# Weight ring and operands placed on 512-byte multiples, narrow weight tiles 192 bytes beside

## The reference

```python
def first_block(x, ...):              # two layers, post-norm
    for layer in range(2):
        mix = dsa_mixer(h, ...) if layer == 0 else hgrn2_mixer(h, ...)
        h = layer_norm(ALPHA * h + mix, ...)
        h = layer_norm(ALPHA * h + swiglu(h, w_gate, w_up, w_down), ...)

def second_block(x, ...):             # one layer, pre-norm
    proj = rms_norm(x) @ w_in         # split into the parts of GLA and of MLA
    y_a = gla_branch(...) @ w_o_gla
    y_b = mla_branch(...) @ w_o_mla
    mixed = (g_a * y_a + g_b * y_b) @ w_out
    x = x + rms_norm(mixed)
    x = x + rms_norm(swiglu(rms_norm(x)))
```

## The kernel before, in words

| tensor | begins at | modulo 512 |
|---|---|---|
| wh | 16512 | 128 |
| stage, wl | 65664 | 128 |
| x_res, xh, xl, ident | 114816, 123008, 131200, 139392 | 128 |
| arena, and hh, hl, oh, ol, mixed_l, lat_h in it | 151904 and on | 352 |
| lat_l | 224224 | 480 |

## Time and profile before

### The profile page before, as it was taken

How to read it: one execution, slowest core, us unless ns; L and a number is a source line. 1 busy time by engine, 2 the same in 40 slices (tenths; PEclk the granted TensorE clock), 3 DMA queues, 4 the chain that set the end, 5 groups by cost and what they waited for, 6 DMA issues and landing times.

```text
span 1100.5 us, 15631 instructions
## 1 busy us (share of the span) xinstructions
PE 1074.5 (98%) x6604; PEld 939.6 (85%) x6604; DVE 403.0 (37%) x730; ACT 554.4 (50%) x741; POOL 775.8 (70%) x201
## 2 busy tenths in 40 slices
PE   8989999999999998999999999999999999999997
PEld 7867888888889997888888899999999988888886
DVE  5984311118743677511110051821184333111103
ACT  6583453443257876444434256465566356443520
POOL 5623698788578751888888868776675767988880
PEclk9999999999999998999999999999999999999999
DMA  9211665555455431575555446544452555555541
GB/s 364 89 39 43 238 222 187 191 191 183 146 208 191 155 116 58 201 259 191 191 180 172 146 159 227 187 160 149 158 188 78 197 185 211 190 184 173 183 150 39
DMA packets 27446, 186.46 MB, mean 169 GB/s; under 512 B 3168, under 2 KB 3424, under 8 KB 5872
## 3 DMA queue, kind: packets, MB, share of 16 engines
q1 hardware_dynamic: 25184, 178.83, 46.7%
q10 hardware_dynamic: 2192, 6.62, 1.8%
HBM read 184.39 MB, written 1.05 MB: 168 GB/s over the span
## 4 chain that ended last, share of the span: by engine, by line
PE 90%; DVE 7%; ACT 1%; DMA 1%; issue 0%; DVEq 0%; SPq 0%
PE ps L382 28%; PE ps L384 27%; PE ps L383 27%; PE ps L1271 1%; PE ps L1432 1%; DVE arena L1046 1%; PE ps L1136 1%; DMA stage<-in_tiles 1%; DVE arena L2306 1%; DVE arena L1062 1%; DVE arena L890 1%; DVE arena L1057 0%; DVE arena L868 0%; PE ps L2141 0%; PE ps L2142 0%
## 5 line engine op out<-in xcount | busy, mean ns | idle before, releaser
L366 POOL TENSOR_TENSOR wl<-stage,wh 128x2048 fp32r<-128x2048 f32 x166 | 763.5, 4621 | 287.0 <-ACT wh L362 256.9
L362 ACT ACTIVATE wh<-stage 128x2048 fp32r<-128x2048 f32 (+1 forms) x167 | 318.0, 1906 | 113.6 <-DMA stage<-in_tiles 112.9
L382 PE MATMUL ps<-wh,xh 128*128 128x512 f32 (+2 forms) x832 | 306.1, 368 | 0.9 <-DVE xl L1095 0.9
L384 PE MATMUL ps<-wh,xl 128*128 128x512 f32 (+2 forms) x832 | 302.0, 363 | 0.0
L383 PE MATMUL ps<-wl,xh 128*128 128x512 f32 (+2 forms) x832 | 301.7, 363 | 0.0
L382 PEld LDWEIGHTS ps<-wh,xh 128*128 128x128 f32 x832 | 157.3, 189 | 24.7 <-DVE xl L1095 1.2
L384 PEld LDWEIGHTS ps<-wh,xl 128*128 128x128 f32 x832 | 157.0, 189 | 24.9
L383 PEld LDWEIGHTS ps<-wl,xh 128*128 128x128 f32 x832 | 157.3, 189 | 23.2
L382 PE MATMUL ps<-xh,wh 128*128 128x256 f32 x464 | 133.1, 287 | 0.8 <-DVE wl L509 0.8
L384 PE MATMUL ps<-xh,wl 128*128 128x256 f32 x464 | 131.3, 283 | 0.0
L383 PE MATMUL ps<-xl,wh 128*128 128x256 f32 x464 | 131.3, 283 | 0.0
(11 more groups left out here) (379 smaller groups left out, 1171.2 us busy)
## 6 DMA issues: line engine op xcount, KB each, us to landing
stage<-in_tiles SPq DMA_DIRECT2D x167, 1024.0 KB, 4.9
arena<-in_ln_g ACTq DMA_DIRECT2D x4, 512.0 KB, 3.6
arena<-in_ln_b ACTq DMA_DIRECT2D x4, 512.0 KB, 4.9
arena<-in_x_t SPq DMA_DIRECT2D x1, 1024.0 KB, 5.5
x_res<-in_x SPq DMA_DIRECT2D x1, 1024.0 KB, 20.8
out<-x_res SPq DMA_DIRECT2D x4, 256.0 KB, 2.1
stage<-in_tiles SPq DMA_DIRECT2D x1, 544.0 KB, 8.9
arena<-in_pre_mix_norm ACTq DMA_DIRECT2D x1, 512.0 KB, 6.7
```

What stands on the lines that cost most here:

```text
L362: nc.scalar.activation(wh[:, ring(n), part], stage[:, ring(n), part], ACT.Copy).then_inc(hi_done, 1)
L366: nc.gpsimd.tensor_tensor(wl[:, ring(n), :], stage[:, ring(n), :], wh[:, ring(n), :].bitcast(F32), ALU.subtract).then_inc(lo_done, 1)
L382: mm(out_, lh, rh, start=start, stop=False, skip_group_check=skip)
L384: return mm(out_, ll, rh, start=False, stop=stop, skip_group_check=skip)
```

## The change

The descriptor scratch is set to 8192 bytes. `until_line` puts gap tensors ahead of `wh`, of `stage`/`wl`, of `xh` and of `arena`, so that each begins at a multiple of 512 bytes; `x_res` and `xl` then do too, and in the arena `hh`, `hl`, `oh`, `ol`, `mixed_l` and `lat_h`; `lat_l` has remainder 128. A slot of the ring has 2176 instead of 2048 elements (8704 bytes). `tile_of` is now the one way to a tile in its slot: tiles whose number is in `narrow` stand 48 elements (192 bytes) into the slot in `stage`, `wh` and `wl`. No instruction is added, removed or moved, and no size of one changes.

```diff
+SCRATCH, LINE = 8192, 512
 TW = 2048
+ROW = TW + 128
+BESIDE = 48
...
+    at = [SCRATCH + 128]
...
         def sb(name, shape, dt=F32):
+            at[0] = -(-(at[0] + math.prod(shape[1:]) * (2 if dt == BF16 else 4)) // 32) * 32
             return ctx.enter_context(nc.sbuf_tensor(name, shape, dt))
...
+        def until_line(offset):
+
+            gap = (offset - at[0]) % LINE
+            if gap:
+                sb("gap%d" % at[0], [P, gap // 4])
+
+        until_line(0)
+        wh = sb("wh", [P, RING, ROW], F32R)
+        until_line(0)
+        with nc.sbuf_tensor("stage", [P, RING, ROW], F32) as stage:
             pass
-        wl = sb("wl", [P, RING, TW], F32R)
+        wl = sb("wl", [P, RING, ROW], F32R)
+
+        def tile_of(ring_of, n, a=0, b=TW):
+
+            return ring_of[:, n % RING, SHIFT[n] + a:SHIFT[n] + b]
+
         x_res = sb("x_res", [P, 2, D])
+        until_line(0)
         xh = sb("xh", [P, KD, T], F32R)
...
+        until_line(0)
         ARENA = 19360
...
+        narrow = {0, 1, 3, *range(t_hx, t_hwo), *range(t_rest, t_ukv), *range(t_gwo, t_out)}
+        SHIFT = [BESIDE if n in narrow else 0 for n in range(FIRST["end"])]
...
-            sp.dma_start(stage[:, ring(n), :], A["tiles"][n]).then_inc(stage_in[ring(n)], 16)
+            sp.dma_start(tile_of(stage, n), A["tiles"][n]).then_inc(stage_in[ring(n)], 16)
...
-                               (wh[:, s, o:o + P], wl[:, s, o:o + P]), (high[:, x0 + k, :], low[:, x0 + k, :]),
+                               (tile_of(wh, n, o, o + P), tile_of(wl, n, o, o + P)), (high[:, x0 + k, :], low[:, x0 + k, :]),
...
-                               (wh[:, s, o:o + 512], wl[:, s, o:o + 512]), start and k == 0, stop and k == 1, skip=True)
+                               (tile_of(wh, n, o, o + 512), tile_of(wl, n, o, o + 512)), start and k == 0, stop and k == 1, skip=True)
...
-    nc = bacc.Bacc("TRN2", target_bir_lowering=False, num_devices=1)
+    nc = bacc.Bacc("TRN2", target_bir_lowering=False, num_devices=1, dynamic_dma_scratch_size=SCRATCH)
```

More of the change, by code:

```diff
@@ L177, in sem @@
             return ctx.enter_context(nc.semaphore(name))
-        wh = sb("wh", [P, RING, TW], F32R)
-        with nc.sbuf_tensor("stage", [P, RING, TW], F32) as stage:
-            pass
-        wl = sb("wl", [P, RING, TW], F32R)
+        def until_line(offset):
[6 more added lines that the diff above has]
+        with nc.sbuf_tensor("stage", [P, RING, ROW], F32) as stage:
+            pass
+        wl = sb("wl", [P, RING, ROW], F32R)
+        def tile_of(ring_of, n, a=0, b=TW):
+            return ring_of[:, n % RING, SHIFT[n] + a:SHIFT[n] + b]
         x_res = sb("x_res", [P, 2, D])
+        until_line(0)
         xh = sb("xh", [P, KD, T], F32R)
@@ L350, in load @@
             if n == 1:
-                sp.dma_start(stage[:, 1, 0:KD * IW], A["tiles"][1, :, 0:KD * IW]).then_inc(stage_in[1], 16)
+                sp.dma_start(tile_of(stage, 1, 0, KD * IW), A["tiles"][1, :, 0:KD * IW]).then_inc(stage_in[1], 16)
                 return
-            sp.dma_start(stage[:, ring(n), :], A["tiles"][n]).then_inc(stage_in[ring(n)], 16)
+            sp.dma_start(tile_of(stage, n), A["tiles"][n]).then_inc(stage_in[ring(n)], 16)
         def ring(n):
@@ L360, in hi @@
             act.wait_ge(stage_in[ring(n)], come[n])
-            part = slice(0, KD * IW if n == 1 else TW)
-            nc.scalar.activation(wh[:, ring(n), part], stage[:, ring(n), part], ACT.Copy).then_inc(hi_done, 1)
+            part = (0, KD * IW if n == 1 else TW)
+            nc.scalar.activation(tile_of(wh, n, *part), tile_of(stage, n, *part), ACT.Copy).then_inc(hi_done, 1)
         def lo(pool, n):
             pool.wait_ge(hi_done, n + 1)
-            nc.gpsimd.tensor_tensor(wl[:, ring(n), :], stage[:, ring(n), :], wh[:, ring(n), :].bitcast(F32),
-                                    ALU.subtract).then_inc(lo_done, 1)
+            nc.gpsimd.tensor_tensor(tile_of(wl, n), tile_of(stage, n), tile_of(wh, n).bitcast(F32), ALU.subtract
+            ).then_inc(lo_done, 1)
         his = [1]
@@ L396, in tile_a @@
             low_ready(pe, n)
-            s = ring(n)
             high, low = src or (xh, xl)
@@ L423, in tile_b @@
                     last = mm3(out_, (xh[:, k, x], xl[:, k, x]),
-                               (wh[:, s, o:o + cols], wl[:, s, o:o + cols]), k == 0, k == kt - 1)
+                               (tile_of(wh, n, o, o + cols), tile_of(wl, n, o, o + cols)), k == 0, k == kt - 1)
             if done:
@@ L431, in rows_t @@
             low_ready(pe, n)
-            s, x = ring(n), slice(t * P, (t + 1) * P)
+            x = slice(t * P, (t + 1) * P)
             high, low = src or (xh, xl)
@@ L508, in first_low @@
         def first_low(n, c):
-            V.tensor_tensor(wl[:, n, c], stage[:, n, c], wh[:, n, c].bitcast(F32), ALU.subtract
+            V.tensor_tensor(tile_of(wl, n, *c), tile_of(stage, n, *c), tile_of(wh, n, *c).bitcast(F32), ALU.subtract
             ).then_inc(first_lo.sem, first_lo.up())
@@ L519, in setup_dve @@
                     dve.wait_ge(hi_done, 1)
-                first_low(0, slice(c * QUARTER, (c + 1) * QUARTER))
+                first_low(0, (c * QUARTER, (c + 1) * QUARTER))
             dve.wait_ge(hi_done, 2)
-            first_low(1, slice(0, KD * IW))
+            first_low(1, (0, KD * IW))
             dve.wait_ge(pos_in, 16)
@@ L602, in setup_x_act @@
             for c in range(4):
-                part = slice(c * QUARTER, (c + 1) * QUARTER)
-                ins = nc.scalar.activation(wh[:, 0, part], stage[:, 0, part], ACT.Copy)
+                part = (c * QUARTER, (c + 1) * QUARTER)
+                ins = nc.scalar.activation(tile_of(wh, 0, *part), tile_of(stage, 0, *part), ACT.Copy)
                 if c < 3:
@@ L673, in dsa_pe @@
                         o = k * 256 + m * P
-                        last = mm3(ps[:, CQ_BANK[m], 0:T], (wh[:, 0, o:o + P], wl[:, 0, o:o + P]),
+                        last = mm3(ps[:, CQ_BANK[m], 0:T], (tile_of(wh, 0, o, o + P), tile_of(wl, 0, o, o + P)),
                                    (xh[:, k, :], xl[:, k, :]), k == 0, k == KD - 1)
@@ L682, in dsa_pe @@
                     last = mm3(ps[:, 1, t * T:t * T + IW], (xh[:, k, x], xl[:, k, x]),
-                               (wh[:, 1, o:o + IW], wl[:, 1, o:o + IW]), k == 0, k == KD - 1)
+                               (tile_of(wh, 1, o, o + IW), tile_of(wl, 1, o, o + IW)), k == 0, k == KD - 1)
             last.then_inc(used, 1)
@@ L692, in query @@
                         last = mm3(ps[:, bank[c], :], (hh[:, 20 + k, x], hl[:, k, x]),
-                                   (wh[:, s, o:o + 512], wl[:, s, o:o + 512]), k == 0, k == 1)
+                                   (tile_of(wh, n, o, o + 512), tile_of(wl, n, o, o + 512)), k == 0, k == 1)
                 return last
@@ L708, in keys_part @@
                     last = mm3(ps[:, 2, t * T:(t + 1) * T], (xh[:, k, x], xl[:, k, x]),
-                               (wh[:, 3, o:o + T], wl[:, 3, o:o + T]), k == 0, k == KD - 1)
+                               (tile_of(wh, 3, o, o + T), tile_of(wl, 3, o, o + T)), k == 0, k == KD - 1)
                 return last
@@ L1260, in product @@
                     last = mm3(ps[:, pair_bank(G, p, t), :], (xh[:, 4 * h + k, x], xl[:, 4 * h + k, x]),
-                               (wh[:, s, o:o + 512], wl[:, s, o:o + 512]), h + k == 0, h == 1 and k == 3, skip=True)
+                               (tile_of(wh, n, o, o + 512), tile_of(wl, n, o, o + 512)), h + k == 0, h == 1 and k == 3, skip=True)
                 return last
@@ L1804, in gla_pe @@
                     flip(pe)
-                w = [y[:, ring(t_rest + 3), k * 256:(k + 1) * 256] for y in (wh, wl)]
+                w = [tile_of(y, t_rest + 3, k * 256, (k + 1) * 256) for y in (wh, wl)]
                 mm3(ps[:, 3, 0:T], (xh[:, k, 0:P], xl[:, k, 0:P]), w, k == 0, k == KD - 1)
@@ L2119, in keys_values @@
                         x = slice(t * P, (t + 1) * P)
-                        w = [y[:, s, k * 1024:(k + 1) * 1024].rearrange("p (h c) -> p h c", h=4)[:, :, MN:MN + MV]
+                        w = [tile_of(y, n, k * 1024, (k + 1) * 1024).rearrange("p (h c) -> p h c", h=4)[:, :, MN:MN + MV]
                              for y in (wh, wl)]
```

## The result

The changed kernel takes 1090.24 us (median of four executions, 1089.73 to 1091.08), the kernel before 1101.78 (1101.34 to 1103.61): ratio 0.9896, 95% interval 0.9882 to 0.991, or 11.5 us less. The forecast was 1091, 10.8 us less.

The account below looks back on a forecast made before the run. TensorE was taken as the bound, busy 1074.5 of 1100.5 us. Terms of -5.9 (wide hh), -4.7 (narrow, after waits) and -0.2 (oh) sum to -10.8 us: 1101.75 to 1091; own range 1088 to 1094, 80% range 1066 to 1102.

Parts of the forecast that it names:

- What bounds the kernel: TensorE, busy 1074.5 of 1100.5 us; a nanosecond taken from every product counts nearly in full, nothing else does.
- the discount of a tenth for gains lost in waits: Narrow tiles before waits in HGRN and around attention: of their 5.2 us only nine tenths, 4.7, counted.
- Wide with hh: 936 wide products, distance 288 to 0: 233.6 to 227.3 ns each, 5.9 us gained; bounds 0 and 16.5 us.
- Wide with xh: 1872 wide products, distance stays 0, remainder 128 to 0: no change; bounds 21 us gain, 11.8 us loss.
- tile_a: 1392 narrow products with xh, distance 0 to 320: 120 to 117 ns each, 4.2 us gained.
- tile_b: 576 narrow products with xh, distance 0 to 192: 120 to 118.2 ns each, 1.0 us gained.
- The bound down to 111 ns: Narrow products' assumed floor, from 136-column products' starts; allowed tile_b up to 5.2 us of gain.
- The floors: Least time between starts: 216 ns for a wide product, from float32 products of 256 columns; 111 ns for a narrow one.
- rival A: Remainder counts too, so wide products with xh also gain: 1059 us in full, 1075 by half; chance 0.24.
- The rest: oh to distance 320 gains 0.2 us; lat products within 0.3 us either way; tile 1 gives 0.
- The rule of the Trainium skill: TensorE's independent read ports for moving operand and weight load: placement would not matter, change worth nothing, 1101.75 us.
- C: Remainder 0 is worst for wide pairs: xh products lose 6.3 ns each, hh gains nothing, 1108.6 us; chance 0.12.

Follow-up runs that it names:

- the scans: Two kernels, the change with a different shift for every tile (coarse, then finer shifts), to show steps at many distances; 1106.74 and 1107.04 us, before 1102.2.

## Why the prediction was right, and where not

**What bounds the kernel.** Right. TensorE's busy time and the span fell by the same 12.6 us, and the gain is spread over the stages in which there are such products. The windows of the HGRN stage, before and after, each from its first narrow product to the first product of the next stage (slightly other edges than in the earlier trace rows), show what waits took:

```profile
328.60:428.80 100.20, 95.93 (x1114) 93.69 (x1112) 64.78 (x105) 74.78 (x135) 58.55 (x13) 0.97 0.42 144
...
327.00:424.40 97.40, 93.70 (x1113) 91.36 (x1112) 64.81 (x105) 74.73 (x135) 58.52 (x13) 0.96 0.43 148
```

TensorE stands idle for 4.3 us before and 3.7 after, and for 26.0 us of the whole span both times. So the discount of a tenth for gains lost in waits is not borne out. The steps of the three classes below add up to 13.3 us and the span gave 12.6; of the difference some 0.3 us are lat products (117.0 to 118.0 ns) and a tenth of a nanosecond on each wide xh product, the rest stays open.

**Wide with hh: 5.9 us forecast.** Right. 233.4 to 226.7 ns on 936 products is 6.3 us, and the kernel without the 192 bytes gained 5.3 us (by its medians). The cause was right as well: it is the distance, as the runs at remainder 128 and with the arena off show.

**Wide with xh: 0 forecast.** Right: 227 ns before, after and at remainder 128.

**tile_a: 4.2 us forecast, to 117 ns.** Right in size, 120 to 117.5 ns on 1392, 3.5 us, but by a step that does not hold. It read 320 off a line between 224 and 352 and took 116.1 ns for 352 from the mix of the lat products. In the scans tile_a takes 119.8 ns at 352, 116.8 at 288 and 120.0 at 256: the values between two measured distances say nothing of one another, and a stream in which distances alternate is no weighted mean of the pure ones. That 320 came out near the 117 ns forecast was luck.

**tile_b: 1.0 us forecast, to 118.2 ns.** Wrong in size; this is the term that was mis-sized. It took 113.9 ns, 576 x 6.1 = 3.5 us. The row it went by, oh at 224, is a good measure of its own distance (118.2 in the scan as well), but 192 has a second, faster pace, which no row of before had, and most of tile_b ran at it. The bound down to 111 ns held it. The 672 fast products of both classes are worth 672 x 4.4 ns = 3.0 us against the slow pace, of a cause that is not known; without them the spans would differ by some 9.6 us instead of 12.6. No term of the sum stood for them, so that the total missed by only 0.7 us (10.8 against 11.5 by the medians) is in part luck.

**The floors.** The 216 ns that the prediction took as the floor of a wide product was read as the time of one float32 product of 256 columns. It is the time of one record: line 739 runs for 8 products and leaves 16 records, two for each, so such a product takes twice as long. The sum did not use this floor, but rival A and the wide bounds did; no run brought a wide product below 226.6 ns over a tile, so what a wide product could do at best stays open.

**The rest.** oh went from 118.2 to 117.8, under 0.1 us. lo, hi and loads cost what they cost, and none came near the path. The prediction's counts leave out 24 products of w_ukv that stream 512 columns of `wh`/`wl` past `lat_h`/`lat_l`; they took 232.9 ns before and 231.7 after, a difference of 0.03 us.

**The rule of the Trainium skill** (TensorE: Matmul & The Clock Gate, Step-by-step: what each phase is for), that loading the next weights does not steal read bandwidth from the running matmul, does not hold here in the sense in which the prediction took it, that placement makes no difference. Moving the arena with the stationary operands `hh` and `hl` from remainder 0 to 224 changes the step from 226.7 to 233.4 ns, and the moves of xl and xh by 32 bytes change it by up to 12 ns. That the two reads of SBUF are where the operands meet is argued from this, and no run shows it directly. Whether float32 products depend on the distance was not looked for.

**The chances.** A and C were given 0.36 together for want of a row at remainder 0. They fell with the result itself, xh at 227 ns at remainder 0, and with the run at remainder 128; the six streams of before had in fact spoken for the distance alone.

## What to carry to other kernels

Where TensorE is the bound and products of type fp32r follow one another, look at the steps from start to start by class of operands. If two classes of one shape have different steps, compare where their moving and stationary operands lie. In this kernel 512-column products were best at a distance of 0 or 256 bytes modulo 512 (7 ns of 233). 256-column products were worst there and gained 2 to 7 ns of 120 at 192 or 320, 3 at 32 or 288, and nothing at 96 or 352. So measure the distance that is meant, since nearby ones are no guide. A moving operand that begins 4 bytes past the stationary one was the worst case for 512-column products, 237.2 ns.

## What was not expected of the hardware

- The step of a wide product hangs on the distance in a pattern of 256 bytes with a grain finer than 32: 228.2 ns at 0, 237.2 at 4, 233.8 at 8, 231.7 at 16, 233.6 at 32, 229.3 at 64.
- Narrow products have two stable paces at one distance, 113.3 and 117.8 ns, which last over tiles; between two executions of one program 2 tiles of 45 changed theirs. Moving the arena alone slowed the pace of some 290 tile_b products that do not read it.
- One load in three out of place by 32 bytes (699.7 ns for three products) costs as much as all three at a distance of 480 would (3 x 233.2).
- GpSimd's, ScalarE's and the DMA's times for a tile did not move with any of the layouts (4617 to 4627 ns, 1906 to 1909 ns, 4.9 us).
